# A fused two-block kernel: first stage with eight load slots, all modulation sums on VectorE, 16 of 31 column tiles in the first pass

## The chip, the cores and the metric

The kernel runs on one core of a Trainium2 chip. The metric is the device time of one execution in microseconds. The three runs of the kernel before took 2594.58 (median), 2593.0 and 2600.59 us.

## The reference, cut to what matters

Two transformer blocks follow each other on 256 tokens of width 2048, all in float32. The change touches the head of the first:

```python
ada = silu(c) @ w_ada + b_ada                    # six parts of 2048: shift_m, scale_m, gate_m, shift_f, scale_f, gate_f
h = rms_norm(x, g_pre_mix) * (1 + scale_m) + shift_m
z = h @ w_in                                     # 2048 x 3920
c_q, c_kv, k_rope, q_g, k_g, v_g, a_g, r_g = split_cols(z, IN_SPLITS)   # 512 256 64 512 512 1024 16 1024
o = concat([mla_mixer(c_q, c_kv, k_rope, ...), gla_mixer(q_g, k_g, v_g, a_g, r_g, ...)]) @ w_out
x = x + gate_m * rms_norm(o, g_post_mix)         # then the FFN with shift_f, scale_f, gate_f
```

The second block (other mixers, another FFN) is not touched.

## The kernel before, in words

**Precision.** Each float32 product is made of three: hi times hi, hi times the rest of x, the rest of w times hi. ScalarE writes the hi part of a weight tile (`split_hi`, L404) into one of four slots of `whi`, VectorE subtracts it from the raw weights and writes the rest (`split_lo`, L416) into `wlo`, TensorE takes three products of 128 x 128 by 256 columns per tile (L441 to L443, L470 to L472).

**Loads.** SyncE (SP) issues all weight loads in order into `raw`, four slots of 1 MB ([128, 2048] float32), called units. Before each it waits until the unit four places back has been used, by the count `raw_done` (two for each unit).

**First pass.** z is made transposed, a tile of 128 columns of w_in at a time, in two passes over k (16 tiles of 128 rows). In the first, each k brings one row unit of w_in with 1744 columns: 14 tiles (one with 80 columns) that fill banks of PSUM over all k (`w_in_row`). Before k can be taken, x must be normed, turned (`pe_turn_rows`, `act_turned`) and modulated with scale and shift of its 128 channels. Each of these sums takes a 1 MB unit of w_ada. The order of units is `FIRST`: scale and shift of four tiles first (`AHEAD` = 4), then a row, a scale, a shift, and so on. A scale sum is one VectorE instruction over the unit times silu(c) on all partitions (`mod_sum`, L429). Shift sums of the tiles in `ON_PE` (0 to 3, 6, 9, 12) are made on TensorE with products of one column (`gemv`, L1855), the other nine on VectorE. ScalarE modulates (L1972), and in its program modulating tile k+4 comes before the hi part of row k+1. VectorE's order per k: low parts of the row, scale, rest of x, shift, rest of x.

**Second pass.** The remaining 17 tiles come in four groups of four (`w_in_chunk`) and a last single one, with a 1 MB unit for four k (n = 0 to 15), each followed by a unit of w_ada for gate_m, which VectorE adds up (L422). `U_WIN` counts the units, `W_WINB` the hi parts. Two side jobs are put in between: the angles of the rotary embedding on VectorE (`dve_angles`, after the low part of n = 0), whose tables ScalarE makes (`act_tables`, with the squares for the latents' norms), and the latents (`pe_latents` after h = 3, which is the end of n = 1, `act_latents` after the first group, `dve_latents` after the low part of n = 6). `z_out` copies finished tiles to SBUF. TensorE's products with ones (L1869) sum gate_m before MLA starts.

At the start ScalarE's queue issues the loads of c (on all partitions), the columns, x, constants and positions; SP issues w_ada units at once. The later stages (MLA, GLA, w_out, FFN, the second block) keep their order.

Of the kernel before, what the change touches and what calls it, by code (L numbers as in the profile page):

```python
# [76 lines left out]
_U_MLA = U_WIN + 2 * 16 + 1  # L77
# [12 lines left out]
W_UQ = W_WINB + 34  # L90
# [24 lines left out]
IN_A = C_QG + GRANK + 7 * P  # L115
AHEAD = 4
ON_PE = (0, 1, 2, 3, 6, 9, 12)


def first_units():  # L120


    units = [(kind, t) for t in range(AHEAD) for kind in ("scale", "shift")]
    for k in range(KT):
        t = k + AHEAD
        if t < KT and t in ON_PE:
            units += [("shift", t), ("row", k), ("scale", t)]
        else:
            units += [("row", k)] + [("scale", t), ("shift", t)] * (t < KT)
    return units  # L130
# [3 lines left out]
FIRST_AT = {item: u for u, item in enumerate(FIRST)}  # L134


def first_done():


    done, n = {}, 0  # L140

    def add(*items):
        nonlocal n
        for item in items:
            n += 2
            done[item] = n

    add(*[("scale", t) for t in range(AHEAD)])
    n += 2 * AHEAD
    done.update({("shift", t): n for t in range(AHEAD)})  # L150
    for k in range(KT):
        t = k + AHEAD
        add(("row", k), *[("scale", t), ("shift", t)] * (t < KT))
    assert n == 2 * len(FIRST)
    return done


FIRST_DONE = first_done()
# [55 lines left out]
def ada_units(w):  # L214
# [10 lines left out]
    for t in ON_PE:  # L225
        units[0, t] = w[:, t * P:(t + 1) * P].reshape(KT, P, P).transpose(1, 0, 2).reshape(P, D)
# [3 lines left out]
def w_in_units(w):  # L230


    first = np.concatenate([w[:, 0:C_QG], w[:, C_AG:C_RG], w[:, C_QG:C_QG + 7 * P]], axis=1)
    second = []
    for parts in WIN_PARTS:
        part = np.concatenate([w[:, c:c + n] for c, n in parts], axis=1)
        second.append(part.reshape(4, 4, P, CW).transpose(0, 2, 1, 3).reshape(4 * P, D))
    second.append(w[:, IN1 - P:IN1].reshape(KT, P, P).transpose(1, 0, 2).reshape(P, D))
    return np.ascontiguousarray(first), np.concatenate(second)


def two_blocks_kernel(nc, a, out):
# [16 lines left out]
    def lay(at, items):  # L259
# [22 lines left out]
    (xs, xf, posi, ang, trig), _ = lay(R1, [  # L282
        ("xs", [P, NT, D], F32), ("xf", [P, KT, T2], F32), ("posi", [P, SEQ], I32), ("ang", [P, SEQ], F32),
        ("trig", [P, 4, SEQ], F32)])
    (gpost, sigc, bcol), _ = lay(top - 8 * D - 4 * NBCOL, [("gpost", [P, D], F32), ("sigc", [P, D], F32), ("bcol", [P, NBCOL], F32)])
    csb = gateF
    (zT,), M0 = lay(R1, [("zT", [P, 32, SEQ], F32)])
# [66 lines left out]
    def landed_at(u, i, nu):  # L354

        return 16 * (u // RING + 1) + i * (16 * nu // RING)
# [66 lines left out]

    def mod_sum(u, to, b, g):


        dve.wait_ge(landed[u % RING], landed_at(u, 0, 0))
        unit = raw[:, u % RING, :]
        return dve.tensor_tensor_reduce(unit, unit, csb[:, :], g, b, ALU.mult, ALU.add, to)  # L429
# [3 lines left out]

    def w_in_row(k):


        w, done = W_WIN + 2 * k, FIRST_DONE["row", k]

        def tile(s, bank, half, t, m=P):
            o, wt = pb[0:m, bank, half * SEQ:(half + 1) * SEQ], slice(t, t + m)  # L440
            mm(o, whi[:, s, wt], xh[:, k, 0:SEQ], start=(k == 0 and half == 0), stop=False, skip_group_check=True)  # L441
# [5 lines left out]
        for n in range(6):  # L447
            tile(s0, n // 2, n % 2, n * P)
        if k:
            tile(s0, 3, 1, 6 * P, ROPE + GRANK).then_inc(used, 1)  # L450
        pe.wait_ge(raw_done, done)
        tile(s1, 3, 0, 0)
        if k == 0:
            tile(s0, 3, 1, 6 * P, ROPE + GRANK)
        for n in range(6):
            last = tile(s1, 4 + n // 2, n % 2, (n + 1) * P)
        last.then_inc(used, 1 if k else 2)

    def w_in_chunk(u, w, b0, behind=None):


        for h in range(8):
            s = (w + h) % SLOTS
            pe.wait_ge(raw_done, 2 * (u + 2 * (h // 2)) + h % 2 + 1)
            for kk in range(2):
                k = 2 * h + kk
                for f in range(4):
                    o = pb[:, b0 + f // 2, (f % 2) * SEQ:(f % 2 + 1) * SEQ]
                    t = slice(kk * CW + f * P, kk * CW + (f + 1) * P)
# [865 lines left out]
    def shift_f(lo, hi):  # L1335

        for n in range(lo, hi):
            mod_sum(U_ADAC[n], mods[:, 2, n:n + 1], b_col(2, n), 1.0).then_inc(raw_done, 2)
# [333 lines left out]
    def _(_sp):  # L1672
# [5 lines left out]
        pe_units = 0  # L1678
        taken = {}
        for u, (kind, t) in enumerate(FIRST):  # L1680
            if u >= RING:
                before = FIRST[u - RING]
                if before in taken:
                    sp.wait_ge(sem("gemv"), taken[before])
                else:
                    sp.wait_ge(raw_done, FIRST_DONE[before])
            if kind == "row":
                src, to = w_in[t * P:(t + 1) * P, :], raw[:, u % RING, 0:IN_A]
            else:
                at = (KT if kind == "scale" else 0) + t  # L1690
                src, to = w_ada[at * P:(at + 1) * P, :], raw[:, u % RING, :]
                if kind == "shift" and t in ON_PE:
                    pe_units += 1
                    taken[kind, t] = pe_units
            sp.dma_start(to, src).then_inc(landed[u % RING], 16)
        for n in range(16):
            load_slab(U_WIN + 2 * n, a["w_in_second"], n * P)
            ada_load(U_WIN + 2 * n + 1, 2, n * P)
        load_slab(U_WIN + 32, a["w_in_second"], 16 * P)
# [149 lines left out]
    def _(_pe):  # L1849

        def gemv(t):
            u = FIRST_AT["shift", t]
            pe.wait_ge(landed[u % RING], landed_at(u, 0, 0))
            for k in range(KT):
# [423 lines left out]
```

## Time and profile before

| what | value |
|---|---|
| runs, median (lowest, highest) | 2594.58 us (2593.0, 2600.59) |
| the profiled execution's own time | 2600.51 us |
| its span | 2598.7 us |
| mean granted TensorE clock | 0.948 |
| PE busy | 2427.3 us (93%) |
| DVE busy | 1547.9 us (60%) |
| ACT busy | 1078.5 us (42%) |
| DMA | 505.31 MB, mean 194 GB/s |

PE is TensorE, PEld its weight loads (which overlap its products), DVE is VectorE, ACT is ScalarE, POOL is GpSimd, SPq is SyncE's queue of DMA issues. Times in a timeline are microseconds from the span's start. The granted clock is 1.00 at 2.4 GHz and 0.50 at 1.2 GHz. A bracket behind a row tells how long the engine was idle before it and what ended that.

### The profile page before, as it was taken

How to read it: one execution, taken by the hardware profiler on the slowest of the kernel's cores; microseconds unless marked ns; L12 is line 12 of the kernel's file. 1: busy time of each engine (PE TensorE's matmuls, PEld its weight loads, DVE VectorE, ACT ScalarE, POOL GpSimd, SP SyncE). 2: the span in 40 equal slices, each digit the busy share in tenths (PEclk: the TensorE clock that was granted, in tenths of full speed). 3: DMA queues.
4: the chain of work that ended last, by engine and by line, in shares of the span. 5: the costliest groups of instructions: out<-in, count | busy, mean ns of one | idle time of the engine just before them, and what ended most of it. 6: DMA issues, size and time to landing. Idle time of an engine off the chain costs nothing.

```text
span 2598.7 us, 42620 instructions
## 1 busy us (share of the span) xinstructions
PE 2427.3 (93%) x16722; PEld 2254.7 (87%) x16722; DVE 1547.9 (60%) x1688; ACT 1078.5 (42%) x1255; POOL 129.2 (5%) x247
## 2 busy tenths in 40 slices
PE   6989976989999999999799999997999999999997
PEld 6979855789998889997699997697999988999975
DVE  3778769865554466754554994345565554565545
ACT  3343443354444334443444434335444433343433
POOL 0000002200000100001200000000000011000011
PEclk9899987989999999999899998598999999999998
DMA  8978826945555567765355551044455555555552
GB/s 313 353 284 317 291 84 261 370 146 186 186 187 185 194 229 272 280 221 174 135 170 173 177 174 52 1 156 137 146 178 189 182 178 194 179 177 188 183 178 97
DMA packets 163094, 505.31 MB, mean 194 GB/s; under 512 B 8126, under 2 KB 12510, under 8 KB 134062
## 3 DMA queue, kind: packets, MB, share of 16 engines
q1 hardware_dynamic: 161248, 496.66, 55.3%
q0 software_dynamic: 752, 3.47, 0.5%
q10 hardware_dynamic: 1008, 4.00, 0.4%
q8 instruction: 57, 0.93, 0.1%
q14 instruction: 29, 0.24, 0.0%
HBM read 502.00 MB, written 2.10 MB: 194 GB/s over the span
## 4 chain that ended last, share of the span: by engine, by line
PE 86%; DVE 8%; ACT 3%; issue 2%; DMA 1%; ACTq 0%; DVEq 0%
PE pb L505 22%; PE pb L491 17%; PE pb L493 17%; PE pb L492 17%; DVE raw L429 2%; DVE wlo L416 1%; PE pb L1855 1%; PE pb L470 1%; PE pb L981 1%; PE pb L603 1%; PE pb L472 1%; PE pb L471 1%; DVE x L1480 1%; PE pb L987 1%; ACT whi L404 1%
## 5 line engine op out<-in xcount | busy, mean ns | idle before, releaser
L416 DVE TENSOR_TENSOR wlo<-raw,whi 128x1024 fp32r<-128x1024 f32 (+2 forms) x750 | 904.5, 1217 | 821.4 <-ACT whi L404 820.9
L404 ACT ACTIVATE whi<-raw 128x1024 fp32r<-128x1024 f32 (+2 forms) x750 | 781.0, 1051 | 1112.6 <-PE pb L493 721.2
L491 PE MATMUL pb<-xh,whi 128*128 128x256 f32 (+2 forms) x3760 | 1067.8, 284 | 9.0 <-DVE accf L1543 3.2
L492 PE MATMUL pb<-xl,whi 128*128 128x256 f32 (+2 forms) x3760 | 1067.4, 284 | 0.0
L493 PE MATMUL pb<-xh,wlo 128*128 128x256 f32 (+2 forms) x3760 | 1066.7, 284 | 0.0
L491 PEld LDWEIGHTS pb<-xh,whi 128*128 128x128 f32 x3760 | 713.9, 190 | 10.8 <-issue 4.0
L492 PEld LDWEIGHTS pb<-xl,whi 128*128 128x128 f32 x3760 | 714.9, 190 | 0.0
L493 PEld LDWEIGHTS pb<-xh,wlo 128*128 128x128 f32 x3760 | 713.5, 190 | 0.0
L505 PE MATMUL pb<-whi,stg 128*128 128x512 f32 x1664 | 449.4, 391 | 16.1 <-DVE xl L1457 8.0
L505 PEld LDWEIGHTS pb<-whi,stg 128*128 128x128 f32 x1664 | 313.6, 189 | 84.2 <-DVE xl L1457 8.7
L505 PE MATMUL pb<-wlo,stg 128*128 128x512 f32 x832 | 257.8, 391 | 0.0
L505 PEld LDWEIGHTS pb<-wlo,stg 128*128 128x128 f32 x832 | 157.2, 189 | 32.8
L429 DVE CUSTOM_DVE_ANT_0 raw<-raw,gateF,bcol 128x2048 f32<-128x2048 f32 x57 | 134.9, 2387 | 0.8 <-DMA raw<-w_ada 0.5
L534 POOL CAST stg<-hTh 128x256 fp32r x88 | 35.7, 405 | 1462.3 <-PE pb L493 1072.8
L441 PE MATMUL pb<-xh,whi 128*128 128x256 f32 (+1 forms) x224 | 69.3, 310 | 20.9 <-DVE wlo L416 13.8
L470 PE MATMUL pb<-xh,whi 128*128 128x256 f32 x256 | 73.8, 288 | 7.5 <-DVE wlo L416 7.5
L2221 DVE SCALAR_TENSOR_TENSOR zT<-upad,colv,zT x180 | 75.7, 480 | 0.0
L471 PE MATMUL pb<-xl,whi 128*128 128x256 f32 x256 | 73.2, 286 | 0.0
L472 PE MATMUL pb<-xh,wlo 128*128 128x256 f32 x256 | 73.2, 286 | 0.0
L442 PE MATMUL pb<-xl,whi 128*128 128x256 f32 (+1 forms) x224 | 68.1, 304 | 0.0
L443 PE MATMUL pb<-xh,wlo 128*128 128x256 f32 (+1 forms) x224 | 68.0, 303 | 0.0
L441 PEld LDWEIGHTS pb<-xh,whi 128*128 128x128 f32 (+1 forms) x224 | 47.4, 212 | 22.2 <-issue 22.2
(375 smaller groups left out, 1779.5 us busy)
## 6 DMA issues: line engine op xcount, KB each, us to landing
raw<-w_ada SPq DMA_DIRECT2D x96, 1024.0 KB, 6.4
raw<-w_ffn_gate SPq DMA_DIRECT2D x44, 1024.0 KB, 5.2
raw<-w_ffn_up SPq DMA_DIRECT2D x44, 1024.0 KB, 5.2
raw<-w_ffn_down SPq DMA_DIRECT2D x44, 1024.0 KB, 4.7
raw<-w_gate SPq DMA_DIRECT2D x44, 1024.0 KB, 5.2
raw<-w_up SPq DMA_DIRECT2D x44, 1024.0 KB, 5.1
raw<-w_down SPq DMA_DIRECT2D x44, 1024.0 KB, 4.7
raw<-w_in SPq DMA_DIRECT2D x40, 1024.0 KB, 5.0
```

The source lines that it names most:

```text
L404: act.activation(to, src, ACT.Copy).then_inc(hi_ready, 1)
L416: dve.tensor_tensor(to, src, hi, ALU.subtract).then_inc(raw_done, 1)
L429: return dve.tensor_tensor_reduce(unit, unit, csb[:, :], g, b, ALU.mult, ALU.add, to)
L441: mm(o, whi[:, s, wt], xh[:, k, 0:SEQ], start=(k == 0 and half == 0), stop=False, skip_group_check=True)
L470: mm(o, whi[:, s, t], xh[:, k, 0:SEQ], start=(k == 0 and f % 2 == 0), stop=False, skip_group_check=True)
L471: mm(o, whi[:, s, t], xl[:, k, 0:SEQ], start=False, stop=False, skip_group_check=True)
L472: last = mm(o, wlo[:, s, t], xh[:, k, 0:SEQ], start=False, stop=(k == KT - 1), skip_group_check=True)
L491: mm(o, whi[:, s, t], xh[:, k, c0:c1], start=(k == 0), stop=False)
L492: mm(o, whi[:, s, t], xl[:, k, c0:c1], start=False, stop=False)
L493: last = mm(o, wlo[:, s, t], xh[:, k, c0:c1], start=False, stop=(k == KT - 1))
L505: last = mm(pb[:, 4 * t + 2 * hh + c, :], stg[:, s, part, t * P:(t + 1) * P], wt[:, ws, c * CW:(c + 1) * CW], start=first and part == 0 an ...
L2221: op = dve.scalar_tensor_tensor(acc, src, wt, acc, ALU.mult, ALU.add)
```

## The change

Loads: while the first units run, there are eight slots: the four of `raw`, the two rows of `xs` (free once x is turned), `sigc` (free once silu(c) is made) and a new buffer `more`. `FIRST_SLOT` says which unit goes where: units 0 to 9 use six slots, units 10 and 11 open the two of `xs`, from unit 12 on each takes the slot of eight places back. SP waits for c before the first of these loads. Each slot has its own semaphore `first_in`.

Sums: `gemv` and `ON_PE` are gone, all scale and shift sums are VectorE's, done in the order of `FIRST`. ScalarE takes the hi part of row k before it modulates tile k+3. x's two halves have semaphores of their own.

Tiles: a row unit of the first pass has 2000 columns: 16 tiles (one with 80 columns), in halves of 848 and 1152. The second pass has 15 tiles, in groups of 4, 4, 4, 3 (`WIN_NF`); the units of the last group are padded in DRAM to full size, so they load as many bytes. The single last tile and its unit are gone. The angles follow the low part of n = 2, the tables the hi part of n = 3, the latents on VectorE the low part of n = 9; `pe_latents` stays behind h = 3.

```diff
-C_W2 = C_QG + 7 * P
-WIN_PARTS = [[(C_W2, CW)], [(C_W2 + CW, CW)], [(C_W2 + 2 * CW, P), (C_RG, 3 * P)], [(C_RG + 3 * P, CW)]]
+C_W2 = C_QG + 9 * P
+WIN_PARTS = [[(C_W2, CW)], [(C_W2 + CW, 3 * P), (C_RG, P)], [(C_RG + P, CW)], [(C_RG + 5 * P, 3 * P)]]
+WIN_NF = (4, 4, 4, 3)
-ON_PE = (0, 1, 2, 3, 6, 9, 12)
+IN_A = C_QG + GRANK + 9 * P
+HALF_A = (C_QG + GRANK + P, 8 * P)
 AHEAD = 4
     units = [(kind, t) for t in range(AHEAD) for kind in ("scale", "shift")]
     for k in range(KT):
+        units += [("row", k)] + [("scale", k + AHEAD), ("shift", k + AHEAD)] * (k + AHEAD < KT)
+EARLY_SLOTS = (0, 1, 2, 3, 6, 7)
+MORE_AT = 10
+def first_slots():
+    slots = []
+    for u in range(len(FIRST)):
+        if u < len(EARLY_SLOTS):
+            slots.append(EARLY_SLOTS[u])
+        elif u < MORE_AT:
+            slots.append(slots[u - len(EARLY_SLOTS)])
+        elif u < MORE_AT + 2:
+            slots.append(4 + u - MORE_AT)
+        else:
+            slots.append(slots[u - 8])
+    return slots
+def slot_before(u, slot):
+    return max([v + 1 for v in range(min(u, len(FIRST))) if FIRST_SLOT[v] == slot], default=0)
...
+    slots1 = [raw[:, n, :] for n in range(RING)] + [xs[:, 0, :], xs[:, 1, :], sigc[:, :], more[:, :]]
+    def row_sum(unit, to, b, g):
+        return dve.tensor_tensor_reduce(unit, unit, csb[:, :], g, b, ALU.mult, ALU.add, to)
+    def first_landed(eng, u):
+        eng.wait_ge(first_in[FIRST_SLOT[u]], 16 * slot_loads(u))
+    def row_halves(k):
+        unit, w = slots1[FIRST_SLOT[FIRST_AT["row", k]]], W_WIN + 2 * k
+        n0, n1 = HALF_A
+        return [((w + hh) % SLOTS, unit[:, lo:lo + n], n) for hh, lo, n in ((0, 0, n0), (1, n0, n1))]
+    def row_hi(k):
+        first_landed(act, FIRST_AT["row", k])
+        for hh, (s, src, n) in enumerate(row_halves(k)):
+            at_least(act, used, W_WIN + 2 * k + hh - SLOTS + 1)
+            act.activation(whi[:, s, 0:n], src, ACT.Copy).then_inc(hi_ready, 1)
...
+        sp.wait_ge(sem("cb_in"), 16)
         for u, (kind, t) in enumerate(FIRST):
+            slot = FIRST_SLOT[u]
+            if slot == 6 and slot_loads(u) == 1:
+                sp.wait_ge(sem("csb_done"), 1)
+            elif u in (MORE_AT, MORE_AT + 1):
+                sp.wait_ge(sem("turned"), KT)
+            at_least(sp, raw_done, 2 * slot_before(u, slot))
+            sp.dma_start(to, src).then_inc(first_in[slot], 16)
...
-        pe.wait_ge(sem("csilu"), 1)
-        for t in range(AHEAD):
-            gemv(t)
         pe.wait_ge(consts_in, 16)
-        pe.wait_ge(raw_done, FIRST_DONE["shift", AHEAD - 1])
         pe_turn_rows(0)
         for k in range(KT):
-            t = k + AHEAD
-            if t in ON_PE:
-                pe.wait_ge(raw_done, FIRST_DONE["shift", max(n for n in ON_PE if n < t)])
-                gemv(t)
             pe.wait_ge(sem("x0_split"), k + 1)
             w_in_row(k)
         for c, (bank, ready) in enumerate(((0, 1), (2, 4), (0, 6), (2, 7))):
             pe.wait_ge(sem("z_out"), ready)
+            w_in_chunk(U_WIN + 8 * c, W_WINB + 8 * c, bank, WIN_NF[c], (3, pe_latents) if c == 0 else None)
...
+        row_hi(0)
+        for t in range(AHEAD):
+            modulate(t)
+        for k in range(1, KT):
             row_hi(k)
-            if k == 0:
-                for t in range(AHEAD):
-                    modulate(t)
-            if k + AHEAD < KT:
-                modulate(k + AHEAD)
+            if k + AHEAD - 1 < KT:
+                modulate(k + AHEAD - 1)
...
+            for n in range(4 * c + 3, min(4 * c + 5, 16)):
+                part_hi(n)
+                if n == 3:
+                    act_tables()
...
+        for t in range(AHEAD):
+            first_sum("scale", t)
+            if t == 2:
+                dve_normed_row(0, 1)
+            first_sum("shift", t)
+            if t == 1:
+                dve_normed_row(0, 0)
         for k in range(KT):
             row_lo(k)
             if k + AHEAD < KT:
-                scale_of(k + AHEAD)
-            for t in (0, 1) if k == 0 else (2, 3) if k == 1 else ():
+                first_sum("scale", k + AHEAD)
+            for t in range(AHEAD) if k == 0 else ():
                 x_rest(t)
             if k + AHEAD < KT:
-                shift_of(k + AHEAD)
+                first_sum("shift", k + AHEAD)
             if k and k + AHEAD - 1 < KT:
                 x_rest(k + AHEAD - 1)
...
-            if n == 0:
+            if n == 2:
                 dve_angles()
-            if n == 6:
+            if n == 9:
                 dve_latents()
             ada_add(U_WIN + 2 * n + 1, adaA, csil[:, n:n + 1])
```

## Rows read from the trace of the kernel before

**Rows 1.** Busy us by stage: length, PE, PEld, DVE, ACT, POOL; clock, DMA, GB/s.

```profile
0.00:288.00 288.00, 241.00 (x1761) 238.07 (x1762) 196.06 (x196) 107.47 (x146) 3.60 (x17) 0.93 0.84 317
...
420.00:2598.00 2178.00, 2089.02 (x14410) 1937.28 (x14410) 1252.89 (x1348) 915.99 (x1004) 116.69 (x222) 0.96 0.53 180
```

**Rows 2.** Whom TensorE waited for until 420 us: total us, times, longest.

```profile
PE pb L1855 <- DVE csil L2107: 18.2, 1, 18.2
PE pb L441 <- DVE wlo L416: 13.8, 7, 3.8
...
PE pb L470 <- DVE wlo L416: 7.5, 2, 4.7
```

**Rows 3.** Timeline of the opening: start, us, engine, line, operation.

```profile
9.77 1.91 ACT L1955 ACTIVATE sigc<-gateF 128x2048 f32<-128x2048 f32 x1 [4.48 <-DMA gateF<-c]
...
18.21 27.51 PE L1855 MATMUL pb<-csil,raw 128*128 128x1 f32 x128 [18.21 <-DVE csil L2107]
...
48.28 4.53 ACT L615 ACTIVATE xf<-pb 128x256 f32<-128x256 f32 x16 [17.47 <-PE pb L603]
...
58.45 0.55 PE L441 MATMUL pb<-xh,whi 128*128 128x256 f32 x1 [7.13 <-DVE xl L2116]
```

**Rows 4.** The table of rows 1 for the opening and the first pass.

```profile
6.00:24.00 18.00, 5.79 (x28) 5.79 (x28) 7.48 (x8) 2.12 (x2) 0.00 (x0) 1.00 1.01 419
...
98.00:156.00 58.00, 45.71 (x330) 44.84 (x331) 45.24 (x49) 20.44 (x30) 0.00 (x0) 0.88 0.96 357
```

**Rows 5.** Timeline of VectorE in the first pass.

```profile
62.92 2.04 DVE L416 TENSOR_TENSOR wlo<-raw,whi 128x848 fp32r<-128x848 f32 x2 [1.96 <-ACT whi L404]
...
102.97 2.04 DVE L416 TENSOR_TENSOR wlo<-raw,whi 128x848 fp32r<-128x848 f32 x2 [1.63 <-ACT whi L404]
104.93 2.40 DVE L429 CUSTOM_DVE_ANT_0 raw<-raw,gateF,bcol 128x2048 f32<-128x2048 f32 x1
...
111.58 2.04 DVE L416 TENSOR_TENSOR wlo<-raw,whi 128x848 fp32r<-128x848 f32 x2 [1.62 <-ACT whi L404]
...
153.99 2.04 DVE L416 TENSOR_TENSOR wlo<-raw,whi 128x848 fp32r<-128x848 f32 x2 [1.62 <-ACT whi L404]
```

**Rows 6.** Timeline of TensorE: first and second pass, begin and end.

```profile
59.22 0.41 PE L441 MATMUL pb<-xh,whi 128*128 128x256 f32 x1
...
59.86 0.41 PE L441 MATMUL pb<-xh,whi 128*128 128x256 f32 x1
...
155.18 0.55 PE L441 MATMUL pb<-xh,whi 128*128 128x256 f32 x1 [3.48 <-DVE wlo L416]
...
176.43 0.28 PE L443 MATMUL pb<-xh,wlo 128*128 128x256 f32 x1
...
287.88 3.60 PE L1869 MATMUL pb<-adaA,kc 128*128 128x512 f32 x8
```

**Rows 7.** DMA issues: KB each, median us from issue to landing.

```profile
raw<-w_down SPq DMA_DIRECT2D x44, 1024.0 KB, 4.7
```

**Rows 8.** The busy table, the last four rows of the first pass.

```profile
158.00:176.00 18.00, 18.00 (x153) 18.00 (x152) 8.64 (x13) 7.57 (x9) 0.00 (x0) 0.99 0.65 234
```

**Rows 9.** Timeline of the second pass: angles, tables, squares, row sums, latents.

```profile
174.15 0.29 DVE L1306 CAST ang<-posi 128x256 f32<-128x256 int32 x1
...
181.58 2.35 DVE L422 SCALAR_TENSOR_TENSOR adaA<-raw,csil,adaA 128x2048 f32<-128x2048 f32 x1
...
184.84 0.42 ACT L1064 ACTIVATE sinT<-trig 128x256 f32<-128x256 f32 x1
...
185.59 1.49 ACT L1068 ACTIVATE sq<-zT 128x1536 f32<-128x1536 f32 x1
...
192.35 1.89 PE L737 MATMUL pb<-sq,kc 128*128 128x256 f32 x8
...
218.88 0.42 DVE L1324 TENSOR_TENSOR kro<-pb,cosT 128x256 f32<-128x256 f32 x1
...
225.89 2.35 DVE L422 SCALAR_TENSOR_TENSOR adaA<-raw,csil,adaA 128x2048 f32<-128x2048 f32 x1
```

More of the change, by code:

```diff
@@ L134, with slot_loads @@
 FIRST_AT = {item: u for u, item in enumerate(FIRST)}
[L137 to L158, printed above, removed]
+EARLY_SLOTS = (0, 1, 2, 3, 6, 7)
[12 more added lines that the diff above has]
+    return slots
+FIRST_SLOT = first_slots()
+def slot_loads(u):
+    return FIRST_SLOT[:u + 1].count(FIRST_SLOT[u])
+def slot_before(u, slot):
+    return max([v + 1 for v in range(min(u, len(FIRST))) if FIRST_SLOT[v] == slot], default=0)
 ADA_AT = [3 * m + 2 for m in range(4)]
@@ L236, in w_in_units @@
         part = np.concatenate([w[:, c:c + n] for c, n in parts], axis=1)
[L237 to L238 removed]
+        n = part.shape[1]
+        unit = part.reshape(4, 4, P, n).transpose(0, 2, 1, 3).reshape(4 * P, 4 * n)
+        second.append(np.pad(unit, ((0, 0), (0, D - 4 * n))))
     return np.ascontiguousarray(first), np.concatenate(second)
@@ L422, in ada_add, with row_lo, tile @@
         dve.scalar_tensor_tensor(acc[:, :], raw[:, u % RING, :], c, acc[:, :], ALU.mult, ALU.add).then_inc(raw_done, 2)
+    def row_sum(unit, to, b, g):
+        return dve.tensor_tensor_reduce(unit, unit, csb[:, :], g, b, ALU.mult, ALU.add, to)
     def mod_sum(u, to, b, g):
         dve.wait_ge(landed[u % RING], landed_at(u, 0, 0))
-        unit = raw[:, u % RING, :]
-        return dve.tensor_tensor_reduce(unit, unit, csb[:, :], g, b, ALU.mult, ALU.add, to)
+        row_sum(raw[:, u % RING, :], to, b, g).then_inc(raw_done, 2)
     def b_col(n, t):
         return bcol[:, KT * n + t:KT * n + t + 1]
+    def first_landed(eng, u):
[9 more added lines that the diff above has]
+            act.activation(whi[:, s, 0:n], src, ACT.Copy).then_inc(hi_ready, 1)
+    def row_lo(k):
+        for hh, (s, src, n) in enumerate(row_halves(k)):
+            dve.wait_ge(hi_ready, W_WIN + 2 * k + hh + 1)
+            dve.tensor_tensor(wlo[:, s, 0:n], src, whi[:, s, 0:n].bitcast(F32), ALU.subtract).then_inc(raw_done, 1)
     def w_in_row(k):
[L437 to L441, printed above, removed]
+        w, done = W_WIN + 2 * k, 2 * FIRST_AT["row", k] + 2
+        def tile(s, n, t, m=P):
+            o, wt = pb[0:m, n // 2, (n % 2) * SEQ:(n % 2 + 1) * SEQ], slice(t, t + m)
+            mm(o, whi[:, s, wt], xh[:, k, 0:SEQ], start=(k == 0 and n % 2 == 0), stop=False, skip_group_check=True)
             mm(o, whi[:, s, wt], xl[:, k, 0:SEQ], start=False, stop=False, skip_group_check=True)
@@ L447, in w_in_row, with w_in_chunk @@
         for n in range(6):
-            tile(s0, n // 2, n % 2, n * P)
-        if k:
-            tile(s0, 3, 1, 6 * P, ROPE + GRANK).then_inc(used, 1)
-        pe.wait_ge(raw_done, done)
-        tile(s1, 3, 0, 0)
-        if k == 0:
[L454 to L459, printed above, removed]
+            last = tile(s0, n, n * P)
+            if k == KT - 1 and n in (3, 5):
+                last.then_inc(sem("row_end"), 1)
+        tile(s0, 6, 6 * P + ROPE + GRANK)
+        tile(s0, 7, 6 * P, ROPE + GRANK).then_inc(used, 1)
+        pe.wait_ge(raw_done, done)
+        for n in range(8, 16):
+            last = tile(s1, n, (n - 8) * P)
+        last.then_inc(used, 1)
+    def w_in_chunk(u, w, b0, nf, behind=None):
         for h in range(8):
@@ L1849, in _ @@
     def _(_pe):
[L1851 to L1854, printed above, removed]
-                last = mm(pb[:, 7, SEQ + t:SEQ + t + 1], raw[:, u % RING, k * P:(k + 1) * P], csil[:, k:k + 1],
-                          start=(k == 0), stop=(k == KT - 1))
-            last.then_inc(sem("gemv"), 1)
-        pe.wait_ge(sem("csilu"), 1)
-        for t in range(AHEAD):
-            gemv(t)
         pe.wait_ge(consts_in, 16)
-        pe.wait_ge(raw_done, FIRST_DONE["shift", AHEAD - 1])
         pe_turn_rows(0)
```

157 lines of the change are left out of this document (51 added, 106 removed).

## The prediction, made before the result was known

> **What bounds the kernel now.** I read the busy table by stage first, then TensorE's waits, then the timelines of the first stage. After 420 us TensorE is busy 2089 of 2178 us [rows 1]; the change touches nothing there, so that part can only move as a block. The loose time is ahead of 288 us: TensorE is busy 241 us, but part of that is not useful work. It waits 18.2 us for silu(c) and then spends 27.5 us on 128 one-column products [rows 2, 3]. Only at 58.45 does the first product of w_in start. In the first pass it waits 13.8 us in all for low parts of w_in, in the second 7.5 us [rows 2]. The reader should see that TensorE's busy share of the first 50 us is misleading: what sets the end of the first pass is the weights' arrival and VectorE's order, not TensorE.
>
> The first pass moves two 1.05 MB w_ada units and one row per k. It gets 357 GB/s at a DMA share of 0.96, while the opening, with more transfers queued, got 419 GB/s [rows 4]. VectorE's step from one row's low part to the next takes 8.61 us (102.97 to 111.58), 1.62 of it idle behind ScalarE [rows 5], since ScalarE modulates behind the shift sum and only then splits the next row. Row 1's split stands at 62.92, row 12's at 153.99: 91.1 us for 11 steps, 8.3 each. Rows 12 to 15 then go back to back on TensorE, from 155.18 to 176.6. The second pass ends at 287.9 with the gate rows [rows 6].
>
> **The opening.** Today c lands at 9.77, beside four w_ada units. In the change SP waits for c, so c has the engines alone. A 1 MB load takes 4.7 us from issue to landing where little is queued [rows 7], so c lands near 6, silu(c) is ready near 10.5, and units start to be issued at 6. The wait queues all SP loads behind it, but the same bytes of the ACT queue (columns, x) use the engines meanwhile. I count bytes, then: 5.05 MB besides the units (c 1.05, gain row 1.05, x 2.1, constants 0.47, the rest 0.38), data from about 2.7 us on (4.7 less 1.05 MB at 0.42 MB/us is 2.2 after the issue at 0.74, rounded up to 2 whole us). At 0.395 MB/us (below: why) unit u3 lands at 2.7 + 9.24/0.395 = 26, u7 at 37, row 0 at 39, scale 4 at 42. VectorE needs 2.35 us a sum, so it follows the landings. Its second x row comes behind scale 2, near 33; the turn is paced by ScalarE's 4.5 us [rows 3], so the two late slots (u10, u11) open near 38. SP stands at that wait, with all later units behind it, but u9 is in transfer until 42, so the cover is 4 us less some 2 of issue latency: cost nothing, and microsecond for microsecond if the turn is over 2 us later. ScalarE then splits row 0 and modulates four tiles (4 us), TensorE starts row 0 at about 45.5 against 58.45, and VectorE splits row 1 at 48.7 against 62.92.
>
> **Seven shift sums move to VectorE, a row of w_in carries 256 more columns.** VectorE's step today is 8.61 - 1.62 = 6.99 us of work with both sums. A row grows from 1744 to 2000 columns: 1.96 us for 1744 (102.97 to 104.93) gives 0.29 more. The idle goes, because ScalarE now splits row k before it modulates tile k+3, and that tile's sum is a whole step old. New step if VectorE is the bound: 7.28. TensorE's row is 16 tiles of 3 products: 153 products in 18.0 us [rows 8] is 0.118 each, 5.7 us a row, under the step; at half clock the products are 0.213 apart (three from 59.22 to 59.86), 10.2 a row [rows 6]. Low-clock spells of some 4 us in the rows of before ended by themselves once TensorE ran back to back, and a row of slack in the four hi slots covers one.
>
> The DMA's step: 2 x 1.049 + 1.024 = 3.12 MB. At 419 GB/s it is 7.45 us, at 357 it is 8.74. Which one holds is the disputed number. Eight slots keep up to five or six units queued as in the opening, which speaks for the high end; today's pass, with a share of 0.96, has little idle to win, which speaks for 357/0.96 = 372. I take 395, the middle of 372 and 419. Step 7.9, so DMA is the bound, VectorE close behind. Row 12 lands at 2.7 + 52.1/0.395 = 134.6 (32 units of 1.049, 13 rows of 1.024, 5.05, and 0.2 of instructions). Plus 2 us for its hi and lo parts: TensorE starts row 12 at 136.6 against 155.18. Four rows are 22.8 us; before, four rows of 4.98 (13 tiles and a narrow one) took 21.4, so 1.5 went to a low clock, which I keep. **End of the first pass 160.9 against 176.6: 15.7 earlier**, with two more tiles done.
>
> The Trainium skill states on "DMA: Bandwidth & Descriptors", section "Where 436 GB/s comes from", that HBM to SBUF loads are held by HBM at about 358 GB/s per core. The pass's 357 [rows 4] looks like that; 419 over 18 us of loads from HBM speaks against it here. By the rule the step would be that of the second rival below.
>
> **The second pass.** 15 tiles instead of 17, each 16 x 3 x 0.1185 = 5.7 us: 96.7 becomes 85.3, and the 32 units (the last four padded to full size) load in 5.3 us per n at 395 GB/s. TensorE needs 5.7 per n in the first three groups, 4.3 in the last; since two n are loaded ahead, I get n = 15 split just before it is wanted, at no cost (up to 3 us without that lead). The latents' row sums, from 192.35 in the profile, take 3.5 as before [rows 9]. The stalls are where the moved steps count:
> - Angles now follow the low part of n = 2. They cost VectorE 7.4 us (174.15 to 181.58) and, further down, the tables and the squares end 2.3 us after them [rows 9]. TensorE's pe_latents still stands behind h = 3, the end of n = 1, and waits for those squares. Low part of n = 2 ends 8.0 us after the first pass's end (hi slot free after 5.7, then 1.06 and 1.2), so the squares are ready at 17.7, TensorE arrives at 11.4: a stall of 6.3. Before, the squares were ready in time and the stall came at n = 1.
> - Latents (7.0 us, 218.88 to 225.89) now follow n = 9, whose hi parts come right after the second group's z_out. Low part ends 4.4 us after n = 7 on TensorE (z_out 1.0, two hi parts of 1.06, lo 1.2); plus 7.0, the gate sum 2.4 and half of n = 10, 1.2, makes 15.0 against the 11.4 at which TensorE wants it: 3.6 of stall.
> Together 9.9 in place of 7.5, with about 4 of low clock behind them as before (111.4 less 96.7, 3.5 and 7.5 leaves 3.7). Sum: 85.3 + 3.5 + 9.9 + 4 = 102.7 against 111.4: **8.7 earlier**. Bounds of the stalls: none (ring ahead further than I think), 12 us less; no better than double, 10 more.
>
> **The rest.** The MLA start waits for x's copy, behind a z_out of 768 columns instead of 256: 0.4 later. One cleared product group and a ring phase of one change nothing that I can find.
>
> Total: 15.7 + 8.7 - 0.4 = 24.0 us. The profiled execution took 2600.5 (span 2598.7), 5.9 above the median of the runs, 2594.6; I take the difference off the median: **2570.6**.
>
> **Rivals.**
> 1. VectorE bound, loads at 419: row 1 at 48.7 plus 11 steps of 7.28 puts row 12 at 128.8, TensorE at 129.8, the pass's end at 154.1, 22.5 earlier. Total 31 us, 2563.7. For it: the opening's 419 with deep queues. Against: the sustained rows are lower.
> 2. Loads stay at 357: row 12 lands at 148.6, the end is 174.9, 1.7 earlier. Total 10 us, 2584.5. For it: the share is already 0.96 and the bytes per step grow. Against: today's queue empties when a slot is freed late.
> 3. Other side: TensorE's clock. The one-column products keep TensorE busy from 18 to 46 today, granted full clock; afterwards it has nothing but transposes until 45, and then waits a quarter of each step. Should it stay at 1.2 GHz through the pass, a row takes 10.2 us, the pass ends at 45.5 + 163 = 208.7, 32 later, total 24 slower, 2618. It decides from 8.8 us a row on, two thirds of the pass at the low level. Against it: row 0 starts after idle today too and was at full clock within 5 us.
> 4. The change's two other slots bring nothing (a late slot, SP in order): VectorE keeps steps of 8.3 + 0.3 from 48.7 on, row 12 at 143.3, the end near 168.6, 8.0 earlier; total 16.5, 2578.
>
> The Trainium skill, "TensorE: Matmul & The Clock Gate", section "HAM oscillation — how this bites in real kernels", has rival 3's mechanism: short bursts with a DMA wait after each start cold every time. The low-clock spells of the profile agree that it occurs here.
>
> **How the numbers follow.** Forecast 0.5; rival 1 0.17; rival 2 0.12; rival 4 0.12; rival 3 0.04; something that leaves it unchanged within 0.3% (7.8 us, about what can be told from no change) 0.05. The range goes from VectorE bound and half of the stalls gone (2558) to the loads at 357 (2585). Faster by over 0.3%: 0.91, same 0.05, slower 0.04.
>
> **What would show it.** Right: the first w_in product near 45 us; VectorE's steps between 7.3 and 7.9 us, without idle behind ScalarE; first pass over at 154 to 165; DMA at 385 to 420 GB/s from 10 to 135; a stall of some 6 us on the squares after n = 1 and one of 3 to 4 after n = 9; 285 to 2600 shifted as a block. Wrong: steps of 8.6 (rival 2 or 4; the DMA share tells which: 1.0 or less), a granted clock of 0.5 through the pass (rival 3), SP waiting on the turn while the DMA stands still, or a later part that does not keep what the first gives.

## The result, and the profile after

The changed kernel takes 2571.59 us (median of 4 runs, 2568.45 to 2574.34), the kernel before 2595.01 (4 runs, 2593.0 to 2600.59). The ratio is 0.9904, 95% interval 0.9885 to 0.9923: 23.4 us faster. The profiled executions took 2574.34 and 2600.51 (spans 2572.5 and 2598.7), 26.2 apart; both lie at the upper end of their kernel's runs, so medians differ by less. Executions of one kernel lie 4 to 15 us apart. The part that the change does not touch varies by nearly as much by itself: from the MLA's start to the end the fourteen profiles of this case take 2294.9 to 2308.8 us, with the same work there. So the stage times inside a profile say more finely than medians where time went. Both are given below.

The busy table by stage of the kernel after (columns as in [rows 1]):

```profile
0.00:290.00 290.00, 221.28 (x1697) 213.31 (x1697) 232.13 (x232) 119.04 (x166) 3.59 (x17) 0.95 0.86 342
420.00:2574.00 2154.00, 2069.04 (x14325) 1920.73 (x14323) 1227.52 (x1326) 906.76 (x995) 112.33 (x216) 0.96 0.53 178
6.00:24.00 18.00, 0.00 (x0) 0.00 (x0) 7.54 (x9) 7.49 (x9) 0.00 (x0) 1.00 1.01 402
50.00:130.00 80.00, 69.46 (x557) 67.94 (x556) 78.26 (x76) 30.50 (x41) 0.00 (x0) 0.97 1.01 421
130.00:150.00 20.00, 18.54 (x157) 18.57 (x158) 11.03 (x11) 10.18 (x12) 0.00 (x0) 1.00 0.52 201
```

The row to look at is 50:130; the kernel before has in the same stretch

```profile
50.00:130.00 80.00, 68.24 (x495) 67.29 (x493) 59.33 (x66) 33.13 (x57) 0.00 (x0) 0.85 0.86 325
```

VectorE is now busy 78.3 of 80 us, where it was 59.3, and the loads run at 421 GB/s, where they ran at 325 here and at 357 in the later stretch of [rows 4]: the first stage now uses two resources nearly fully, where before it used neither. Up to the gate rows TensorE is busy 197 us (0 to 258.2) against 241 before (0 to 287.8), for the same products of w_in; 38 of these 44 us are the one-column products, which are gone.

Whom TensorE waited for until 300 us (as [rows 2]):

```profile
PE pb L632 <- DVE xs L617: 31.8, 2, 30.1
PE pb L471 <- DVE wlo L462: 12.0, 8, 2.0
PE pb L471 <- DVE xl L2118: 7.3, 1, 7.3
PE pb L766 <- ACT sq L1097: 6.6, 1, 6.6
PE pb L499 <- DVE wlo L421: 3.6, 1, 3.6
PE pb L792 <- issue: 3.6, 1, 3.6
```

The timeline of ScalarE, then of TensorE, in the kernel after (start, us, engine, line, operation, idle before):

```profile
5.60 1.91 ACT L1958 ACTIVATE sigc<-gateF 128x2048 f32<-128x2048 f32 x1
...
34.26 4.64 ACT L644 ACTIVATE xf<-pb 128x256 f32<-128x256 f32 x16 [15.51 <-PE pb L632]
...
170.62 1.48 ACT L1097 ACTIVATE sq<-zT 128x1536 f32<-128x1536 f32 x1
```

```profile
45.55 0.55 PE L471 MATMUL pb<-xh,whi 128*128 128x256 f32 x1 [7.30 <-DVE xl L2118]
...
154.05 0.28 PE L473 MATMUL pb<-xh,wlo 128*128 128x256 f32 x1
...
172.25 3.75 PE L766 MATMUL pb<-sq,kc 128*128 128x256 f32 x8 [6.61 <-ACT sq L1097]
...
258.24 3.67 PE L1886 MATMUL pb<-adaA,kc 128*128 128x512 f32 x8 [0.22 <-DVE adaA L427]
...
265.46 0.36 PE L792 MATMUL pb<-xh,whi 128*128 128x256 f32 x1 [3.55 <-issue]
```

From such rows, the starts of the stages in us:

| | before | after | earlier by |
|---|---|---|---|
| first product of w_in | 58.45 | 45.55 | 12.9 |
| second pass starts | 176.6 | 154.2 | 22.4 |
| gate rows (L1869, L1886) | 287.9 | 258.2 | 29.6 |
| MLA (L763, L792) | 292.6 | 265.5 | 27.1 |
| w_out (L505, L534) | 426.3 | 398.6 | 27.7 |
| span | 2598.7 | 2572.5 | 26.2 |

So everything is gained ahead of the gate rows, 2.5 us are lost between them and the MLA, and the rest moves as a block. VectorE in one step of the first pass (the timeline, to be held against [rows 5]):

```profile
77.86 2.31 DVE L462 TENSOR_TENSOR wlo<-raw,whi 128x976 fp32r<-128x976 f32 x2 [0.35 <-ACT whi L456]
80.09 2.41 DVE L432 CUSTOM_DVE_ANT_0 raw<-raw,gateF,bcol 128x2048 f32<-128x2048 f32 x1
82.42 0.08 DVE L432 DVE_READ_ACCUMULATOR2_ANT mods<- 128x1 f32 x1
82.42 2.35 DVE L432 CUSTOM_DVE_ANT_0 raw<-raw,gateF,bcol 128x2048 f32<-128x2048 f32 x1
84.69 0.08 DVE L432 DVE_READ_ACCUMULATOR2_ANT mods<- 128x1 f32 x1
84.69 0.42 DVE L2118 TENSOR_TENSOR xl<-xf,xh 128x256 fp32r<-128x256 f32 x1
85.23 2.31 DVE L462 TENSOR_TENSOR wlo<-xs,whi 128x976 fp32r<-128x976 f32 x2
```

Both sums, the rest of x and a wider low part in 7.37 us, where [rows 5] has 8.61 with 1.62 idle. Low parts start at 48.65 (row 1) and 130.14 (row 12): 7.41 a step, which is 3.12 MB at 421 GB/s. The section on the change gives the halves of a row as 848 and 1152 columns; these rows show 976, which leaves 1024 of the 2000 for the other half. The sum used 2000 in all and is not touched.

### The profile page after: what moved, and what is told of

Its sections match the earlier page's. It is cut to its first block, busy times and chain, and to the rows that moved or that the text cites. A ratio compares the mean times of both kernels' runs of the same rounds, so it can differ in the third digit from the quotient of the medians.

```text
span 2572.5 us, 42120 instructions
## 1 busy us (share of the span) xinstructions
PE 2380.5 (93%) x16498; PEld 2206.6 (86%) x16498; DVE 1563.3 (61%) x1696; ACT 1077.6 (42%) x1252; POOL 130.8 (5%) x247
## 4 chain that ended last, share of the span: by engine, by line
PE 85%; DVE 7%; DMA 3%; ACT 2%; issue 2%; DVEq 0%; ACTq 0%
PE pb L534 22%; PE pb L520 18%; PE pb L522 18%; PE pb L521 18%; DMA xs<-w_in 1%; DMA raw<-w_ada 1%; PE pb L1010 1%; DVE raw L432 1%; DVE x L1509 1%; PE pb L1016 1%; PE pb L632 1%; PE pb L499 1%; PE pb L501 1%; PE pb L500 1%; DMA sigc<-w_in 1%
## 5 line engine op out<-in xcount | busy, mean ns | idle before, releaser
L421 DVE TENSOR_TENSOR wlo<-raw,whi 128x1024 fp32r<-128x1024 f32 (+1 forms) x716 | 868.1, 1222 | 788.9 <-ACT whi L409 788.8
L409 ACT ACTIVATE whi<-raw 128x1024 fp32r<-128x1024 f32 (+1 forms) x716 | 749.1, 1054 | 1111.7 <-PE pb L522 720.7
L534 PE MATMUL pb<-whi,stg 128*128 128x512 f32 x1664 | 450.3, 392 | 16.0 <-DVE xl L1486 7.9
L534 PEld LDWEIGHTS pb<-whi,stg 128*128 128x128 f32 x1664 | 314.2, 189 | 83.9 <-DVE xl L1486 8.6
L534 PE MATMUL pb<-wlo,stg 128*128 128x512 f32 x832 | 257.7, 391 | 0.0
L534 PEld LDWEIGHTS pb<-wlo,stg 128*128 128x128 f32 x832 | 157.3, 189 | 33.0
L432 DVE CUSTOM_DVE_ANT_0 raw<-raw,gateF,bcol 128x2048 f32<-128x2048 f32 x49 | 115.9, 2386 | 8.9 <-DMA raw<-w_ada 8.9
L632 PE MATMUL pb<-kc,xs 128*128 128x128 f32 x128 | 29.5, 392 | 58.1 <-DVE xs L617 58.1
L632 PEld LDWEIGHTS pb<-kc,xs 128*128 128x128 f32 x128 | 22.0, 203 | 60.4 <-issue 56.3
L472 PE MATMUL pb<-xl,whi 128*128 128x256 f32 (+1 forms) x256 | 73.7, 288 | 0.0
L473 PE MATMUL pb<-xh,wlo 128*128 128x256 f32 (+1 forms) x256 | 73.5, 287 | 0.0
L499 PE MATMUL pb<-xh,whi 128*128 128x256 f32 x240 | 68.4, 285 | 3.6 <-DVE wlo L421 3.6
L501 PE MATMUL pb<-xh,wlo 128*128 128x256 f32 x240 | 67.9, 283 | 0.0
```

The source lines that it names most:

```text
L409: act.activation(to, src, ACT.Copy).then_inc(hi_ready, 1)
L421: dve.tensor_tensor(to, src, hi, ALU.subtract).then_inc(raw_done, 1)
L499: mm(o, whi[:, s, t], xh[:, k, 0:SEQ], start=(k == 0 and f % 2 == 0), stop=False, skip_group_check=True)
L501: last = mm(o, wlo[:, s, t], xh[:, k, 0:SEQ], start=False, stop=(k == KT - 1), skip_group_check=True)
L534: last = mm(pb[:, 4 * t + 2 * hh + c, :], stg[:, s, part, t * P:(t + 1) * P], wt[:, ws, c * CW:(c + 1) * CW], start=first and part == 0 an ...
L632: turn = pt(pb[:, k % 8, c:c + r], src[:, k * P:(k + 1) * P], kc[0:r, K_ID:K_ID + r])
```

## Experiments

Theories at the start. **A**: the gain comes from the eight slots, which keep the loads dense. **B**: it comes from ScalarE's order (split row k before modulating the next tile), which takes VectorE's 1.6 us of idle out of each step. **C**: silu(c) first gives the opening. The kernel before ran again beside each of the four groups of experiments, and each ratio is to the before of its own group: 2596.6 (slots, old order, row sums after h = 7), 2594.8 (order alone, no wait for c, no padding, rearranged), 2596.0 (sums alone, both, rearranged with six slots and no wait) and 2596.7 (the last run).

**Slots.** Four slots, then six, in place of eight:

```diff
-EARLY_SLOTS = (0, 1, 2, 3, 6, 7)
-MORE_AT = 10
+EARLY_SLOTS = (0, 1, 2, 3)      # six slots: this line as it was
+MORE_AT = 999
```

> The changed kernel with only the four slots of raw in the first stage (unit u in slot u mod 4), all else as changed. Theory A (more transfers queued keep the DMA engines full): the rate from 50 to 130 us falls from 421 GB/s to 370 to 390, VectorE's step from row to row from 7.41 us to 8.1 to 8.4, row 12's low part moves from 130.1 to 138 to 141, the end of the first pass from 154 to 163 or so, the whole kernel is 8 to 11 us slower than the changed one (about 2581). Theory B (the order on ScalarE made the gain, the slots add nothing): the step stays at 7.6 or less, the total within 2 us of the changed kernel.

> The changed kernel with six slots throughout the first stage (raw, sigc, more), without the two rows of xs. Theory A: four transfers of 1 MB in flight are enough to keep the engines full, so six slots give nearly what eight give: step 7.4 to 7.6 us, total 0 to 2 us slower than the changed kernel. Theory B: no difference from four slots or from eight. A third outcome, a step halfway between four and eight slots (7.8 to 8.0), would say that every slot counts.

Measured: four slots 2572.53 (ratio to before 0.9905, 0.9887 to 0.9922), six 2571.59 (0.9898, 0.988 to 0.9917), eight 2571.59. The busy table of four slots:

```profile
50.00:130.00 80.00, 66.27 (x522) 64.78 (x521) 76.54 (x75) 30.38 (x42) 0.00 (x0) 0.96 1.00 410
```

410 GB/s and steps of 7.60 us with four slots; 421 and 7.34 with six. The first pass ends at 156.7 with four and 153.5 with six, 154.2 with eight. Theory A is refuted: the slots are worth 2.5 us at the end of the first pass and nothing that the whole time shows. One of the five executions with six slots took 2559.65, 12 below their median; its profile has the MLA start at 263.0, only 2.5 before the changed kernel's, so the rest of that came in the part that no run changes.

**ScalarE's order.** The changed kernel with the old order:

```diff
-        row_hi(0)
-        for t in range(AHEAD):
-            modulate(t)
-        for k in range(1, KT):
+        for k in range(KT):
             row_hi(k)
-            if k + AHEAD - 1 < KT:
-                modulate(k + AHEAD - 1)
+            if k == 0: ...               # modulate tiles 0 to 3
+            if k + AHEAD < KT:
+                modulate(k + AHEAD)
```

> The changed kernel with ScalarE's order of before: tile k+4 is modulated ahead of the hi part of row k+1. Theory (order): VectorE again idles 1.6 us per step behind ScalarE, the step is 7.2 + 1.6 = 8.8 us, row 12's low part at 146 or so, the first pass ends 15 to 16 us later, total about 2587. Rival (DMA alone is the bound, VectorE's idle is absorbed): step 7.4 to 7.6, total within 2 us of the changed kernel.

Measured: 2592.97 (0.9979, 0.9968 to 0.999). One exchange of two calls takes back some 20 of the 23 us (3.6 us are left against the before of its group). That is more than the theory's 15 to 16: its step is 8.98 us, row 1's low part is 2.4 later, row 12's low part stands at 149.9, the first pass ends at 173.9 and the MLA starts at 285.1, each of the last three 19.7 later than in the changed kernel. Its busy table, and whom ScalarE waited for from 60 to 150 us; then the same waits in the changed kernel:

```profile
50.00:130.00 80.00, 62.45 (x462) 60.97 (x461) 65.13 (x63) 25.68 (x36) 0.00 (x0) 0.91 0.99 392
...
ACT xh L1969 <- DVE mods L432: 60.4, 10, 6.0
```

```profile
ACT whi L456 <- DMA raw<-w_in: 23.6, 5, 5.1
ACT whi L456 <- DMA sigc<-w_in: 9.0, 2, 4.5
ACT whi L456 <- DMA xs<-w_in: 8.9, 2, 4.4
ACT whi L456 <- PE pb L473: 6.1, 4, 1.8
```

This pair is the cleanest reading of the case. In the old order ScalarE waits 6.0 us in each step for the sum that VectorE has just made, modulates, splits, and VectorE waits for the split: a circle through both engines, 8.98 us long. In the new order ScalarE waits for the loads: the circle is cut, and the transfers set the step. The 392 GB/s of the old order is an average of two parts. Until 100 us the loads run ahead into the eight slots, at 412 to 425 GB/s; from 100 to 130 they get only the slots that the circle frees, 332 to 355 GB/s, and the DMA share is still 0.94 to 0.98. The time from issue to landing tells the two states apart: from 100 to 130 us a unit takes 5.2 to 7.4 us in the old order and 16.3 to 16.6 in the changed kernel, where loads queue behind each other.

**The order alone, the sums alone, both.** The order in the kernel before, with its four slots and its products of one column; then in the kernel before the shift sums 6, 9 and 12 moved to VectorE (four stay on TensorE ahead of the rows; in the kernel before these three units stand ahead of their row and its scale, and the edit also puts them behind both); then both:

```diff
-ON_PE = (0, 1, 2, 3, 6, 9, 12)
+ON_PE = (0, 1, 2, 3)             # sums alone, and both
```

> The kernel before with one edit: ScalarE takes the hi part of row k ahead of modulating tile k+3 (the changed kernel's order); four slots, one-column products and 14 tiles as before. Theory (the order is the main cause in the first pass): VectorE's idle of 1.6 us per step goes, the step is 7.0 to 7.2 us instead of 8.3, row 12's low part moves from 154.0 to 138 to 141, total 13 to 15 us faster than before (about 2582). Rival (the order helps only with the other parts, since the transfers stayed at 357 GB/s): step 8.0 or more, total within 4 us of before.

> The kernel before with the shift sums 6, 9 and 12 moved from TensorE to VectorE (four stay on TensorE, ahead of the rows); ScalarE's order stays the old one. Theory (with the old order each step that has both sums on VectorE costs 8.6 us, and the three steps whose sum TensorE takes cost 6.4): three cheap steps become dear ones, row 12's low part moves from 154.0 to about 157 to 160, and the kernel is 2 to 6 us slower than before, near 2598. Rival (the one-column products among the rows are what holds the loads back, whatever ScalarE's order): row 12's low part near 146, 6 to 9 us faster than before, near 2587.

> The same with ScalarE's new order as well (next row split first, then the tile modulated). Theory (the new order pays only where no unit's slot waits for TensorE's place in its own order): the step goes from 7.8 us with the order alone to 7.3 (VectorE's 6.99 of work, 2.99 MB at 410 GB/s), row 12's low part comes near 141, first pass over near 162, 14 us earlier than before, and the time is near 2582, 8 or more below the order alone. Rival (the order alone brought all it can with four slots): no more than 2 us from the order alone's 2590.

| | median | ratio, 95% interval | row 12's low part | first pass ends | MLA starts |
|---|---|---|---|---|---|
| before | 2595.0 | | 154.0 | 176.6 | 292.6 |
| order alone | 2590.5 | 0.998, 0.9968 to 0.9991 | 146.0 | 167.1 | 281.3 |
| sums alone | 2599.7 | 1.0015, 1.0004 to 1.0027 | 157.8 | 178.9 | 293.2 |
| both | 2584.2 | 0.9955, 0.9939 to 0.9971 | 141.9 | 164.3 | 280.0 |

The order alone brought 4 us where 13 to 15 were expected: a miss, and the next two runs were made for it. They fell as their theory had it (3.7 slower where 2 to 6 stood, 2584.2 where 2582 stood). By the medians the parts sum to nothing and together give 12, so some 11 us belong to the pair. The profiles agree in sign, with smaller sizes: at the end of the first pass 9.4 earlier, 2.3 later, and 12.3 earlier for both, 5 for the pair; at the MLA's start 11.3 earlier, 0.6 later and 12.6 earlier, 2 for the pair. In the profiles, then, most of the gain is the order's own. Which size is nearer, these runs leave open. What the products of one column cost beside the new order is visible in the order alone. Whom SP's queue waited for from 60 to 150 us, and one of the turns of one-column products:

```profile
SPq L1695 <- DVE mods L429: 39.2, 17, 3.3
SPq L1695 <- DVE wlo L416: 18.6, 9, 3.6
SPq L1695 <- PE pb L1855: 13.9, 3, 5.3
...
94.07 3.63 PE L1855 MATMUL pb<-csil,raw 128*128 128x1 f32 x32
...
50.00:130.00 80.00, 68.68 (x505) 67.89 (x504) 62.91 (x68) 32.65 (x55) 0.00 (x0) 0.85 0.87 343
```

Unit and slot are held until TensorE, which works in order and has the row ahead of them to finish, comes to these products; SP, also in order, issues nothing for up to 5.3 us. Three times in the pass the loads fall behind; ScalarE waits up to 8.1 us at once for a row of w_in there, and up to 5.4 with both edits (56.2 and 52.0 in all, so the sum of these waits hardly tells). With these sums on VectorE the SP wait for L1855 is absent and the loads run at

```profile
50.00:130.00 80.00, 60.42 (x443) 58.82 (x442) 73.83 (x76) 35.16 (x59) 0.00 (x0) 0.89 0.91 363
```

(the run with both), and the step is 7.41 us instead of 7.76. In the old order the same shift sums on TensorE are useful: they make three steps short. So moving the sums pays only with the new order; the new order pays by itself too, 4 us by the medians and 11 in the profiles.

**silu(c) first.** SP's wait for c taken out:

```diff
-        sp.wait_ge(sem("cb_in"), 16)
         for u, (kind, t) in enumerate(FIRST):
```

> The changed kernel without SyncE's wait for c: the first w_ada units are issued at once, beside c. Theory (the opening is held by its bytes): c lands at 9 to 10 us instead of 5.5, the first scale sum starts 1 to 3 us later than 16.7, but units are then waiting; row 0 starts within 2 us of 45.55 and the total is within 3 us of the changed kernel. Rival (silu(c) first is what the opening gained by): row 0 starts 4 us or more later, total 4 to 8 us slower.

Measured: 2572.67 (0.9908, 0.9889 to 0.9926), row 0 at 44.3 against 45.5, first pass over at 153.3. The wait is worth nothing here; theory C is refuted. What is left for the opening's 12.9 us is that the 128 one-column products [rows 3] no longer stand ahead of the transposes: "both" still has them and starts row 0 at 57.9, while four slots (45.4) and the old order (45.8) hardly move it. This is shown by elimination; no run moved these four sums alone.

"Both" is 12.6 us slower than the changed kernel, and beside the opening it lacks the two tiles moved to the first pass. No run moved them alone either. What the profiles show is that the step stays at 7.41 us though a row is 256 columns wider, and that the second pass, up to the gate rows, takes 104.1 us instead of 111.0.

**Second pass.** The latents' row sums placed after h = 7; and the last group's units loaded without their padding:

```diff
-... WIN_NF[c], (3, pe_latents) if c == 0 else None)
+... WIN_NF[c], (7, pe_latents) if c == 0 else None)     # the row sums
...
+                elif WIN_NF[n // 4] < 4 and u == U_WIN + 2 * n:      # the padding
+                    m = WIN_NF[n // 4] * 4 * P
+                    load(u, src[:, 0:m], raw[:, u % RING, 0:m])
```

> The changed kernel with the latents' row sums on TensorE behind h = 7 (end of n = 3) in place of h = 3 (end of n = 1). Theory: the wait of 6.6 us for the squares and some 2 us of low clock behind it go, a wait of 1 to 2 us for the low part of n = 3 comes (it stands behind the angles on VectorE), so the second pass and the total are 5 to 7 us faster than the changed kernel. Rival: the second pass is held by VectorE and the ring, the time is given back before its end: total within 2 us.

> The changed kernel with the last four units of the second pass loaded at their real width (1536 of 2048 columns, 0.79 MB instead of 1.05). Theory (the end of the second pass waits for loads: w_uq arrives 4.6 us after ScalarE wants it): MLA's first product comes 1.5 to 3 us earlier than at 265.5, total 1 to 3 us faster. Rival: the loads are hidden, no difference.

Measured: 2565.24 (0.988, 0.986 to 0.99), MLA at 258.0: the stall on the squares is gone, TensorE waits 2.0 us more for low parts (L499) in its place, and with the low clock behind the stall gone too (1.00 from 171 to 181 us, where the changed kernel has 0.69) the second pass ends 6.2 us earlier, 6.4 by the medians. The theory had 5 to 7. Without the padding: 2572.11 (0.9901, 0.988 to 0.9922), MLA at 265.1 against 265.5; a quarter fewer bytes in the w_in units of the last group bring nothing that can be told, so the rival holds.

**A better version.** The stalls of the second pass taken out together: angles on VectorE in the opening's idle 6.5 us, tables and squares right after the hi part of n = 2, row sums after h = 5, the latents' steps on VectorE in three pieces, positions and constants loaded ahead of x, no padding:

```diff
-... (3, pe_latents) if c == 0 else None)
+... (5, pe_latents) if c == 0 else None)
...
         dve.wait_ge(sem("csilu"), 1)
+        dve_angles()
...
-            if n == 2:
-                dve_angles()
-            if n == 9:
-                dve_latents()
+            if n in LAT_AT:              # (6, 10, 11)
+                dve_latents[LAT_AT.index(n)]()     # rope, reciprocal, scaling
...
         part_hi(2)
+        act_tables()
```

> The changed kernel with the stalls of the second pass taken out by moves: constants and positions loaded ahead of x, the angles in VectorE's idle stretch at 10 to 17 us, tables and squares behind the hi part of n = 2, the latents' row sums behind h = 5, the latents' work on VectorE in three pieces (after n = 6, 10 and 11), the last four units unpadded. Theory: the waits of 6.6 and 3.6 us and their low clock (3 to 4 us) go, and 2 us at the end: 12 to 15 us faster than the changed kernel, about 2558. Rival (the ring and VectorE hold the second pass): no more than the 6 us that moving the row sums alone gave.

Measured: 2561.41 (0.9861, 0.9842 to 0.988), 10.2 us below the changed kernel, less than the 12 to 15 expected; in the profile the MLA starts at 251.6, 13.8 earlier. TensorE's waits on L499 fall to 1.7 us, those on L766 are gone, and the granted clock is 1.00 over the whole second pass (0.95 in the changed kernel).

The last two put six slots into it, first without the wait for c, then with it:

> The rearranged second pass of the run before, with six slots in the first pass and without the wait for c ahead of the units. If the stage times of those single changes add: first pass over near 153.3 instead of 154.2, row 0 one us earlier, and the rest as there: 2560.4, 1 us below the rearranged kernel's 2561.4, which this measurement can hardly tell. If the lower numbers of six slots were more than chance: near 2555.

> The rearranged kernel with six slots, and with the wait for c ahead of the units back in place (the run before had six slots and no wait). Theory (without the wait the positions' load landed at 23.7, behind the units, and the angles held all sums behind it on VectorE): row 0 back near 46, low part of row 12 near 130, first pass over near 154, MLA near 251, time 2558 to 2562. Rival (the six slots cost the time, since the sums' units come later): row 0 stays near 57, time near 2567.

Measured: 2567.03 (0.9887, 0.987 to 0.9903) without, 2559.25 (0.9845, 0.9829 to 0.9861) with. The first missed both expectations: row 0 came at 57.5. The second had row 0 at 46.0, row 12's low part at 130.0 and the first pass over at 154.0, as its theory said, and the MLA at 253.4 instead of 251. VectorE's timeline and the DMA issues of its opening, and its first pass:

```profile
23.73 0.29 DVE L1335 CAST ang<-posi 128x256 f32<-128x256 int32 x1 [6.34 <-DMA posi<-positions]
...
31.16 2.41 DVE L432 CUSTOM_DVE_ANT_0 raw<-raw,gateF,bcol 128x2048 f32<-128x2048 f32 x1
...
posi<-positions ACTq DMA_DIRECT2D x1, 128.0 KB, 20.8
...
50.00:130.00 80.00, 65.08 (x516) 63.65 (x515) 80.00 (x82) 37.49 (x54) 0.00 (x0) 0.94 1.01 412
```

128 KB took 20.8 us to land beside four units, the angles waited for them, and VectorE's first sum, behind the angles, came at 31.2 instead of 17.8. With the wait for c the same load, issued in the same place, lands in 6.4 us, since the units are issued only from 5.5 us on. So the wait for c does nothing where no engine needs a small load early, and is worth 7.8 us by the medians (11.4 at row 0) where VectorE's first work needs one. The run without the wait also shows the floor that VectorE sets: 80.00 of 80 us busy and steps of 7.16 us, the loads being ahead. The version with six slots and the wait beats both kernels of this case by 12 and 37 us; against the rearranged kernel with eight slots the 2 us are within what the runs scatter.

## Why the prediction was right, step by step

The forecast was 2570.6, the median 2571.6. The mechanism held; two sizes were off and cancel in part. That forecast and median lie 1 us apart is luck: the first pass ended 6.7 us earlier than predicted, the second pass and the MLA's head took back 1.4 and 2.1, and the rest is scatter between executions.

- **Opening.** Row 0 predicted at 45.5, measured 45.55; row 1's low part 48.7, measured 48.65. The turn opened the late slots at 38.3 (38 predicted) without starving the loads. c landed at 5.5, silu(c) was ready at 9.8. Right, but the credit for it belongs to the products removed, not to c's early load.
- **VectorE's step.** "The idle goes": right, 7.16 us of work against 7.28 predicted, and the run with the old order shows that most of the gain hangs on it: 19.7 of the 27.1 us at the MLA's start.
- **Rate of the loads: the term mis-sized.** 395 GB/s was the middle between 372 and 419; measured 421. Steps of 7.41 instead of 7.9 make 5.4 us over 11 steps. Rival 1's end of the first pass, 154.1, came out (154.2), but not by rival 1's cause. It let VectorE bound the step at 7.28 with the loads at 419, and by the prediction's own line 419 GB/s is a step of 7.45, so the loads would have bound it; measured is 7.41, and ScalarE's waits show rows arriving late. Its row 12 is 1.3 us early, and the low clock that it keeps for the last rows, which did not come, makes that good. The reason given for the high end, more units queued, carried little: four slots reach 410. And "little idle to win" was read from one stretch: the share is 0.96 from 98 to 156 us, but 0.86 from 50 to 130. What had kept the rate down was slots freed late, above all by ScalarE's circle; SP also stood 11.9 us in three waits for the products in TensorE's order.
- **First pass over** at 154.2 against 160.9 predicted: 5.4 by the rate, nearly all of the rest because the last four rows had no low clock (1.00 from 130 to 150), where 1.5 was kept for it.
- **Second pass.** 104.1 us against 102.7 predicted. Stalls: 6.6 on the squares (6.3 predicted), 3.6 after the latents (3.6 predicted). Moving the row sums removed the first, the rearranged kernel both.
- **Head of the MLA: the term too small.** 7.2 us from the gate rows to L792 against 4.7 before; 0.4 more was predicted, 2.5 came. The prediction had looked at the width of z's copy and not at what stands ahead of it. ScalarE's program has the hi parts of w_uq (L406) ahead of the last group's z_out (L1994):

```profile
257.74 0.63 ACT L406 ACTIVATE whi<-raw 128x512 fp32r<-128x512 f32 x1 [4.57 <-DMA raw<-w_uq]
...
261.41 0.79 ACT L1994 ACTIVATE zT<-pb 128x768 f32<-128x768 f32 x1
```

  TensorE is through with z near 258, but its copy waits for w_uq's load and then for four splits until 261.4; x's hi part (262.1), its rest on VectorE (263.6) and the MLA (265.5) follow. Before, TensorE's work on the single last tile, until 287.9, covered the same splits, which began at 283.3. It is the order of the first pass again: new work ahead of an item that is already there. No run exchanges the two. What delays the load of w_uq was tried only by taking off the padding, which is not it (257.3); its slot is freed by VectorE's low part at 248.5 and it lands 9.2 us later.
- **Sum.** 24.0 predicted, 26.2 in the profiles, 23.4 by the medians. The profiled execution after was 2.8 above its median and the one before 5.5 above its own, which is why the two differ. One slip in the opening does not matter: 2.2 after 0.74 is 2.9 and not 2.7, and the 2.2 was rounded down, not up.
- **Rivals.** 2 (loads at 357): refuted. 3 (clock): refuted, 0.97 from 50 to 130 while TensorE idled 10.5 of the 80 us in gaps of 2.0 or less; of sixteen slices of 5 us thirteen are at 1.00, so it did not start cold after each wait. 4 (the extra slots bring nothing) was true of the slots and false of its consequence, since the steps did not need them.

The Trainium skill's page "DMA: Bandwidth & Descriptors", section "Where 436 GB/s comes from", has HBM hold one core's loads at about 358 GB/s. With one core at work the trace does not agree: 421 GB/s over 80 us. The Trainium skill's page "HBM Reference", section "Specifications (TRN2)", says that a core streaming alone measures about 425 and that 358 is the share with both cores at work. The trace agrees with that, with 421, and it would have chosen the high end.

## What to carry to other kernels

Where two engines hand work to each other in each step, look for the circle: if A waits for what B has just made, and B then waits for A, let A first do the item that is already there; here that exchange was worth 20 us, and four more buffers nothing that the whole time shows. Work that holds a load's slot should sit on an engine that reaches it soon, and an edit that helps only together with another has to be tried with it. A rate below the peak in a profile whose DMA share is near 1 is no proof that the transfers are the bound.

## What the hardware showed that was not expected

- A DMA share of 0.96 went with 357 GB/s (before), 0.98 with 355 (old order, 110 to 120 us), 1.00 with 410 and 1.01 with 421. The share says that something was under way, not how much was moved. The time from issue to landing of a 1 MB load was the better sign (100 to 130 us): 16.3 to 16.6 us with eight slots where the loads set the step, 5.2 to 7.4 with eight slots where they did not. It says something only where there are more slots than the loads need: with four it is 7.0 to 7.7 in the changed kernel and in the kernel before alike.
- Four slots of 1 MB, each reloaded as soon as it is used, sustain 410 GB/s over 80 us; six and eight 421.
- 128 KB of positions took 20.8 us to land when issued just after four units of 1 MB had begun, and 6.4 in the same place with the units held back until c had landed. In the changed kernel, where it comes behind x and the constants, it took 19.9 and nothing waited for it.
